# A two-block network on one core: some of TensorE's work moved to other places in its order, and one GpSimd product held back

## The chip, the cores and the metric

The kernel runs on one core of a Trainium2 chip. The metric is the device time of one execution in microseconds (us): the median of three runs before was 1147.24 (1146.61 to 1147.52). Everything is in one program with one instruction stream for each of five engines: TensorE (PE, and PEld for its weight loads), VectorE (DVE), ScalarE (ACT), GpSimd (POOL) and SyncE (SP), which issues most of the loads. The streams meet only through semaphores.

## What is computed

256 tokens of 1024 features pass through two blocks. The first is a mixer with four branches and a feed-forward; the second is an HGRN2 mixer, a feed-forward, an RG-LRU mixer and a feed-forward. Before each part stands an RMS norm, and after the last a final one. Cut to what matters here:

```python
def first_block(x, ...):
    h = rmsnorm(x, norm_mix)
    x = x + hybrid_mixer(h, ...)          # mamba2, moba, forgetting, sliding window; gates; @ w_out
    x = x + swiglu(rmsnorm(x, norm_ffn), w_gate, w_up, w_down)
    return rmsnorm(x, norm_final)

def second_block(x, ...):
    hn = rmsnorm_2(x, norm_mix[0]); x = x + hgrn2_mixer(hn, w_in, lb, norm_w, w_out)
    x = x + swiglu_2(rmsnorm_2(x, norm_ffn[0]), ffn_w_in[0], ffn_w_out[0])
    hn = rmsnorm_2(x, norm_mix[1]); x = x + rglru_mixer(hn, ...)
    x = x + swiglu_2(rmsnorm_2(x, norm_ffn[1]), ffn_w_in[1], ffn_w_out[1])
    return rmsnorm_2(x, norm_final)

# in hgrn2_mixer, at the end of each head:
#   o = o * rsqrt(mean(o*o)) * norm_w;  o = o * silu(g);  return o @ w_out
```

## The kernel before

**Matmuls in three parts.** Every fp32 product with a large weight is made of two halves of each operand: a high part (whi, hh, eh, gh, ch) rounded to fp32r and the rest (wlo, hl, el, gl, cl). TensorE computes high times high, weight's rest times high and weight's high times activations' rest into one PSUM bank. The weights stream through three slots in units of up to 1 MB. A unit j is loaded by SP in two halves into raw, ACT writes whi from it (L944), DVE (L1342), or for the second halves in the feed-forwards GpSimd (L1912), writes wlo, and then SP may load unit j+3. ACT may write whi of a slot only when TensorE has used the unit before in it (`used`).

**Two forms.** `still` (L480) keeps a weight tile in the array and moves the 256 tokens; a unit of 256 columns is two calls of 24 matmuls, L491 (high), L494 (weight's rest), L497 (activations' rest), in that order for each half of the unit. `moving` (L500) keeps the activations in the array and moves 512 columns of weights: L508 (high), L511 (weight's rest), L514 (activations' rest).

**A norm between two products.** `add_product` (L579) adds a product to x. Its four banks are 4, 6 (first columns) and 5, 7 (second columns) or the other way by token. Its last three units are run for the first two banks and then for the last two. DVE adds a bank to x and multiplies x by the norm's row into hn (`by_row`, L1354); ACT squares x for the mean; GpSimd makes the power; the factor per token is applied later. `transposes(c, e)` (L545) turns one half of hn, eight transposes (L554), into two banks; ACT copies them to hh (L976) and DVE writes hl (L1366). The first half is turned before the last unit's second banks, the second half in `project_pair` (L557). That function runs the two units behind a norm in halves: both units with features 0 to 511 (`part` 0), then `transposes(1, e)`, then unit one with features 512 to 1023, then the spreading of the norm's factors (diag by DVE at L1372, two matmuls with the identity at L574, copied by ACT at L984), then unit two. e numbers the norms: 2 before the first feed-forward, 3 before HGRN2 ("third norm", two norms in one), 5 and 7 before the other feed-forwards, 6 before the RG-LRU; 4 is HGRN2's own output norm.

**The start.** TensorE projects unit ("xbc", 0) (L640 to L649), then turns the 120 rows of small parameters (L656, "columns"), whose loads GpSimd issues, then projects the units ("xbc", 1 to 3). ACT copies the turned columns to vec (L1036), which the convolution on ACT (L1028) and DVE (L1472, L1474) needs.

**HGRN2.** Behind the projections of f and q, `level(j, i)` (L847, L842) computes score products for four pairs of heads at nine levels; between two levels of one pair DVE multiplies q and k by decays (L1749, L1756, L1757; they add one to s_q) and writes the selected scores (L1762). GpSimd multiplies the gates sgt by the output norm's weights in `scaled_gate` (L2059), four products. `turn_outputs` (L873) turns the mixed outputs og for `add_product(("ho",), ...)`: pieces 0 and 1 before it, pieces 2 and 3 inside it, before unit 2's first banks (`before_last`).

## Time and profile before

| | |
|---|---|
| median of three runs | 1147.24 us (1146.61 to 1147.52) |
| the profiled execution | 1146.94 us |
| its span, first to last instruction | 1145.7 us |
| PE (matmul) busy | 1126.2 us, 98% |
| DVE busy | 661.0 us, 58% |
| ACT busy | 575.6 us, 50% |
| POOL busy | 296.6 us, 26% |
| DMA, mean | 181 GB/s |
| mean granted TensorE clock | 0.998 |

Busy time is summed per engine; waits are idle time in front of an instruction, put down to the semaphore that came last. Matmuls are pipelined and the ends of their records are modelled, so two matmuls in the records overlap; the distance from one start to the next is what a matmul costs. A group of instructions in the timeline has one line: start, time from its first start to its last end, engine and line, tiles, count, and in brackets the engine's idle time before it with what ended it.

### The profile page before, as it was taken

What the parts mean: (1) busy time and instruction counts of PE and PEld (TensorE: products, weight loads), DVE (VectorE), ACT (ScalarE), POOL (GpSimd) and SP (SyncE); (2) the same over time, 40 slices, a digit from 0 to 9 for tenths busy, and PEclk for the clock granted to TensorE, in tenths of its full rate; (3) what the DMA queues carried; (4) which work ended last, traced back from release to release, by engine and by line L of the source; (5) the groups of instructions that cost most, each with busy time, mean ns of one, the idle gap of its engine ahead of it and who ended that gap; (6) DMA issues with size and microseconds to landing.
All of it is one profiled execution on the core that took longest, in us unless ns stands there. A gap on an engine that the chain in (4) does not pass through costs nothing.

```text
span 1145.7 us, 19296 instructions
## 1 busy us (share of the span) xinstructions
PE 1126.2 (98%) x8117; PEld 1046.1 (91%) x8117; DVE 661.0 (58%) x1034; ACT 575.6 (50%) x881; POOL 296.6 (26%) x193
## 2 busy tenths in 40 slices
PE   8999999999999999999999999999999999999997
PEld 6999989999989999888998889999889989999986
DVE  6655765677656454337897666434337796534324
ACT  6646555555435644436642445444435855444432
POOL 2023100000005444423321105444420002444440
PEclk9999999999999999999999999999999999999999
DMA  8679474544646666655553348665555354766550
GB/s 269 225 215 334 145 244 133 181 154 135 199 147 201 186 188 200 201 184 161 174 165 112 110 147 261 218 186 187 198 184 176 102 178 138 221 187 192 189 185 37
DMA packets 155152, 207.48 MB, mean 181 GB/s; under 512 B 9471, under 2 KB 128409, under 8 KB 155066
## 3 DMA queue, kind: packets, MB, share of 16 engines
q1 hardware_dynamic: 151274, 193.11, 53.5%
q0 software_dynamic: 3792, 13.15, 3.4%
q8 instruction: 64, 1.05, 0.4%
q14 instruction: 22, 0.18, 0.0%
HBM read 205.01 MB, written 4.24 MB: 183 GB/s over the span
## 4 chain that ended last, share of the span: by engine, by line
PE 89%; DVE 6%; ACT 2%; DMA 1%; issue 1%; POOL 0%; SPq 0%; DVEq 0%; ACTq 0%; POOLq 0%
PE bank L491 18%; PE bank L494 18%; PE bank L497 18%; PE bank L514 9%; PE bank L511 9%; PE bank L508 9%; PE bank L847 2%; DVE wlo L1342 2%; PE bank L773 1%; PE bank L783 1%; PE bank L795 1%; DMA area<-in_hgrn_lb 1%; PE bank L554 1%; DVE uc L1472 0%; ACT whi L944 0%
## 5 line engine op out<-in xcount | busy, mean ns | idle before, releaser
L1342 DVE TENSOR_TENSOR wlo<-raw,whi 128x1024 fp32r<-128x1024 f32 x275 | 339.3, 1261 | 227.7 <-ACT whi L944 226.7
L944 ACT ACTIVATE whi<-raw 128x1024 fp32r<-128x1024 f32 x362 | 360.7, 1044 | 110.4 <-PE bank L514 102.9
L1912 POOL TENSOR_TENSOR wlo<-raw,whi 128x1024 fp32r<-128x1024 f32 x87 | 223.2, 2566 | 256.0 <-ACT whi L944 256.0
L491 PE MATMUL bank<-hh,whi 128*128 128x256 f32 x1784 | 286.3, 281 | 1.7 <-ACT hh L976 1.7
L494 PE MATMUL bank<-hh,wlo 128*128 128x256 f32 x1784 | 281.7, 279 | 0.0
L497 PE MATMUL bank<-hl,whi 128*128 128x256 f32 x1784 | 281.5, 279 | 0.0
L491 PEld LDWEIGHTS bank<-hh,whi 128*128 128x128 f32 x1784 | 241.7, 188 | 6.7 <-issue 5.5
L494 PEld LDWEIGHTS bank<-hh,wlo 128*128 128x128 f32 x1784 | 240.8, 188 | 0.0
L497 PEld LDWEIGHTS bank<-hl,whi 128*128 128x128 f32 x1784 | 240.6, 188 | 0.0
L1919 POOL TENSOR_TENSOR st<-st,half 128x1 f32<-128x1 f32 x18 | 10.3, 580 | 334.6 <-DVE st L1359 310.3
L508 PE MATMUL bank<-whi,gh 128*128 128x512 f32 x264 | 81.5, 390 | 0.0
L514 PE MATMUL bank<-whi,gl 128*128 128x512 f32 x264 | 81.4, 389 | 0.0
L511 PE MATMUL bank<-wlo,gh 128*128 128x512 f32 x264 | 81.3, 389 | 0.0
L1171 ACT ACTIVATE sg<-sg 128x512 f32<-128x512 f32 x33 | 20.9, 632 | 95.6 <-DVE sg L1389 95.6
L1175 ACT ACTIVATE gh<-sg 128x512 fp32r<-128x512 f32 x33 | 20.8, 630 | 86.0 <-DVE sg L1705 86.0
L514 PEld LDWEIGHTS bank<-whi,gl 128*128 128x128 f32 x264 | 49.5, 188 | 10.4
L511 PEld LDWEIGHTS bank<-wlo,gh 128*128 128x128 f32 x264 | 49.5, 188 | 10.3
L508 PEld LDWEIGHTS bank<-whi,gh 128*128 128x128 f32 x264 | 49.2, 188 | 10.0
L1705 DVE TENSOR_TENSOR sg<-sg,bank 128x512 f32<-128x512 f32 x33 | 22.7, 687 | 57.4 <-PE bank L497 55.3
L1389 DVE TENSOR_TENSOR sg<-bank,bc_f 128x512 f32<-128x512 f32 x33 | 22.7, 688 | 43.9 <-PE bank L497 43.9
L969 ACT ACTIVATE bank<-x_sb 128x512 f32<-128x512 f32 x28 | 16.8, 598 | 56.5 <-DVE x_sb L1411 29.9
L1707 DVE TENSOR_TENSOR gl<-sg,gh 128x512 fp32r<-128x512 f32 x33 | 30.8, 932 | 23.3 <-ACT gh L1175 23.3
(308 smaller groups left out, 1224.7 us busy)
## 6 DMA issues: line engine op xcount, KB each, us to landing
raw<-in_ffn_w_in SPq DMA_DIRECT2D x88, 512.0 KB, 3.8
raw<-in_w_in SPq DMA_DIRECT2D x72, 512.0 KB, 5.0
raw<-in_ffn_w_out SPq DMA_DIRECT2D x44, 512.0 KB, 3.3
raw<-in_hgrn_w_in SPq DMA_DIRECT2D x32, 512.0 KB, 4.4
raw<-in_w_ffn_gate SPq DMA_DIRECT2D x22, 512.0 KB, 4.4
raw<-in_w_ffn_up SPq DMA_DIRECT2D x22, 512.0 KB, 4.3
raw<-in_w_ffn_down SPq DMA_DIRECT2D x22, 512.0 KB, 3.5
raw<-in_w_branch SPq DMA_DIRECT2D x16, 512.0 KB, 4.6
```

The lines of the kernel that those rows point to most:

```text
L491: T.matmul(out, wh[:, i, c], xh[:, k, :], start=first and (i, k) == pairs[0], stop=False)
L494: T.matmul(out, wl[:, i, c], xh[:, k, :], start=False, stop=False)
L497: t = T.matmul(out, wh[:, i, c], xl[:, k, :], start=False, stop=last and (i, k) == pairs[-1])
L508: T.matmul(out, xh[:, k, r], wh[:, i, c], start=first and i == 0, stop=False)
L511: T.matmul(out, xh[:, k, r], wl[:, i, c], start=False, stop=False)
L514: tok = T.matmul(out, xl[:, k, r], wh[:, i, c], start=False, stop=last and i == len(ks) - 1)
L847: tok = T.matmul(banks[b][:, 128 * (2 * h + t):128 * (2 * h + t) + 128], kj[:, h, c], qj[:, h, c], start=True, stop=True)
L944: A.activation(half_of(whi, j, h), half_of(raw, j, h), ACT.Copy).then_inc(s_hi[j % NS][h], 1)
L1342: V.tensor_tensor(half_of(wlo, j, h), half_of(raw, j, h), half_of(whi, j, h).bitcast(f32), ALU.subtract).then_inc(s_lo[j % NS][h], 1)
L1389: V.tensor_tensor(dst, two(bank_of("col", *key)[:, :]), bc[:, :].rearrange("p (o t) -> p o t", o=1).broadcast_to([128, 2, 256]), ALU.mult) ...
L1707: V.tensor_tensor(gl[:, 2 * j:2 * j + 2, :], two(s), gh[:, 2 * j:2 * j + 2, :].bitcast(f32), ALU.subtract).then_inc(s_gl, 1)
L1912: G.tensor_tensor(half_of(wlo, j, 1), half_of(raw, j, 1), half_of(whi, j, 1).bitcast(f32), ALU.subtract).then_inc(s_lo[j % NS][1], 1)
```

## The change

TensorE's order is changed at six points, and one wait is put before one GpSimd product. No matmul, transpose or DMA is added or removed.

1. Columns: the turning of the parameter rows is called after the first 24 matmuls of unit ("xbc", 1) instead of before them.
2. First rests: in w_out's product the first unit runs its L508 and L511 parts for all four banks, then the L514 parts for all four.
3. Norms' second turning: `transposes(1, e)` stands behind unit one's first half instead of behind both units' first halves (all five norms).
4. Third norm's factors: for e = 3 the spreading moves from before unit two's second half into it, behind the L494 part of its first 128 columns.
5. Last pieces: `turn_outputs((2, 3))` stands between the two banks of unit 1's first pass instead of before unit 2's.
6. GpSimd's last of the four gate products waits until s_q has its last value, that is, until DVE has done the last level's multiplications.

```diff
@@ still
+                    if inside is not None and of_half:
+                        inside()
                     for i, k in of_half:
                         tq.wait_ge(*lo(k))
                         t = T.matmul(out, wh[:, i, c], xl[:, k, :], ...)
@@ moving: each of the three loops now under "if 0 in parts", "if 1 in parts", "if 2 in parts"
@@ project_columns
                 for m in range(units[j][2] // 128):
                     t = still(...)
+                    if between is not None and m == 0:
+                        between()
@@ project_pair
                             tok = still(..., i0=4 * part, first=part == m == 0, last=part == m == 1,
+                                        inside=(lambda: spread_factors(e)) if part == i == 1 and m == 0 and e == 3 else None)
                         tok.then_inc(s_full[bs[i]], 1)
                         used[j, part] = ...
-                        if part == 1 and i == 0:
-                            turn(("fac", e), 4)
-                            tq.wait_ge(s_diag, SPREAD[e] + 2)
-                            tq.wait_ge(*free(("fac", e)))
-                            for t in range(2):
-                                tok = T.matmul(banks[4][:, 128 * t:128 * t + 128], diag[:, t, :], ident[:, :], start=True, stop=True)
-                            tok.then_inc(s_full[4], 1)
-                    if part == 0:
-                        transposes(1, e)
+                        if part == i == 0:
+                            transposes(1, e)
+                        if part == 1 and i == 0 and e != 3:
+                            spread_factors(e)
@@ add_product
                 for n in range(n_units - 3):
-                    part(n, 0)
-                    part(n, 1)
+                    for parts in ((0, 1), (2,)) if rests_last else ((0, 1, 2),):
+                        part(n, 0, parts)
+                        part(n, 1, parts)
                 for n in range(n_units - 3, n_units):
-                    if before_last is not None and n == n_units - 2:
-                        before_last()
-                    part(n, 0)
+                    part(n, 0, between=inside_second if n == n_units - 3 else None)
@@ start
             for j in range(1, 4):
-                project_columns(("xbc", j), 0)
+                project_columns(("xbc", j), 0, turn_columns if j == 1 else None)
@@ calls
-            add_product(("wo",), 4, eh, el, *of_norm(1), 2)
+            add_product(("wo",), 4, eh, el, *of_norm(1), 2, rests_last=True)
-            add_product(("ho",), 4, eh, el, *of_norm(4), 5, before_last=lambda: turn_outputs((2, 3)))
+            add_product(("ho",), 4, eh, el, *of_norm(4), 5, inside_second=lambda: turn_outputs((2, 3)))
@@ scaled_gate (GpSimd)
                 for t in range(2):
+                    if g2 == t == 1:
+                        gq.wait_ge(s_q, max(lev_q.values()))
                     gq.wait_ge(*evac("tok", "hg", g2, t))
```

## Rows read from the trace of the kernel before

**Rows 1.** The page: busy time of each engine, and its costliest TensorE line.
```profile
PE 1126.2 (98%) x8117; PEld 1046.1 (91%) x8117; DVE 661.0 (58%) x1034; ACT 575.6 (50%) x881; POOL 296.6 (26%) x193
...
L491 PE MATMUL bank<-hh,whi 128*128 128x256 f32 x1784 | 286.3, 281 | 1.7 <-ACT hh L976 1.7
```

**Rows 2.** Timeline at the start (start us, us, engine line, tiles, count, idle before).
```profile
14.60 4.62 DVE L1342 TENSOR_TENSOR wlo<-raw,whi 128x1024 fp32r<-128x1024 f32 x4
...
19.17 0.33 PE L656 MATMUL bank<-ident,area 120*128 120x120 f32 x1 [1.38 <-DMA area<-in_hgrn_lb]
...
19.53 0.27 ACT L1036 ACTIVATE vec<-bank 128x120 f32<-128x120 f32 x1 [1.11 <-PE bank L656]
```

**Rows 3.** Timeline at the unit z1.
```profile
44.79 2.36 DVE L1342 TENSOR_TENSOR wlo<-raw,whi 128x1024 fp32r<-128x1024 f32 x2 [1.65 <-ACT whi L944]
...
49.14 1.09 PE L511 MATMUL bank<-wlo,hh 128*128 128x512 f32 x4
```

**Rows 4.** Timeline of TensorE at w_out's first unit.
```profile
312.13 0.63 PE L511 MATMUL bank<-wlo,eh 128*128 128x512 f32 x2
313.95 0.74 PE L514 MATMUL bank<-whi,el 128*128 128x512 f32 x2 [1.19 <-DVE el L1662]
...
315.92 0.62 PE L508 MATMUL bank<-whi,eh 128*128 128x512 f32 x2
```

**Rows 5.** Timeline at the fourth norm (e = 5), one of five alike.
```profile
680.22 1.28 DVE L1354 TENSOR_TENSOR hn<-x_sb,wrow 128x512 f32<-128x512 f32 x2
...
681.78 0.63 PE L491 MATMUL bank<-hh,whi 128*128 128x256 f32 x4
...
684.61 1.04 PE L554 MATMUL bank<-ident,hn 128*128 128x128 f32 x8
...
686.73 0.63 PE L494 MATMUL bank<-hh,wlo 128*128 128x256 f32 x4
```

**Rows 6.** Timeline at the third norm (e = 3) and the first levels.
```profile
525.09 1.28 DVE L1354 TENSOR_TENSOR hn<-x_sb,wrow 128x512 f32<-128x512 f32 x2
...
525.97 0.63 PE L491 MATMUL bank<-hh,whi 128*128 128x256 f32 x4
...
529.43 1.08 ACT L976 ACTIVATE hh<-bank 128x512 fp32r<-128x512 f32 x2 [1.09 <-PE bank L554]
...
532.12 1.83 POOL L2068 MEMSET Ss<- 128x2048 f32 x1
...
532.63 1.47 DVE L1372 COPY diag<-st 128x128 f32<-128x128 f32 x2
...
534.16 0.71 PE L574 MATMUL bank<-ident,diag 128*128 128x128 f32 x4 [0.74 <-DVE diag L1372]
...
542.35 0.63 ACT L1203 ACTIVATE qT<-qT 128x512 f32<-128x512 f32 x1 [0.81 <-DVE qT L1389]
...
550.06 1.16 PE L847 MATMUL bank<-qT,kT 128*128 128x128 f32 x8 [0.15 <-DVE qT L1749]
```

**Rows 7.** One line's instructions (min/median/max ns), then the timeline at the last level.
```profile
L1756 DVE TENSOR_TENSOR qT<-qT,tot x24: 397/412/1431, 560.5 to 649.5; 128x256 f32<-128x256 f32 x24
...
649.38 1.27 POOL L2059 TENSOR_TENSOR sgt<-sgt,nw 128x512 f32<-128x512 f32 x1 [1.52 <-ACT sgt L1226]
649.51 1.42 DVE L1756 TENSOR_TENSOR qT<-qT,tot 128x256 f32<-128x256 f32 x1 [2.84 <-PE bank L847]
...
651.32 0.71 PE L842 MATMUL bank<-qT,kT 128*128 128x128 f32 x4 [0.98 <-DVE kT L1757]
```

**Rows 8.** Timeline of TensorE at the last pieces' turning.
```profile
662.95 1.03 PE L880 MATMUL bank<-ident,og 128*128 128x128 f32 x8
...
664.87 0.62 PE L511 MATMUL bank<-wlo,eh 128*128 128x512 f32 x2
```

**Rows 9.** Timeline in the first feed-forward: a split on GpSimd and its first reader.
```profile
346.18 2.95 POOL L1912 TENSOR_TENSOR wlo<-raw,whi 128x1024 fp32r<-128x1024 f32 x1 [5.90 <-ACT whi L944]
...
351.16 0.63 PE L494 MATMUL bank<-hh,wlo 128*128 128x256 f32 x4
```

More of the change, by code:

```diff
@@ L478, in next_bank, with still @@
                 return rot_banks[0][(rotation[0] - 1) % len(rot_banks[0])]
-            def still(out, j, m, xh, xl, ks, hi, lo, i0=0, first=True, last=True):
+            def still(out, j, m, xh, xl, ks, hi, lo, i0=0, first=True, last=True, inside=None):
                 wh, wl = whole(whi, j), whole(wlo, j)
@@ L498, in still, with moving @@
                 return t
-            def moving(out, j, t, xh, xl, ks, c0, n, hi, lo, first=True, last=True):
+            def moving(out, j, t, xh, xl, ks, c0, n, hi, lo, first=True, last=True, parts=(0, 1, 2)):
                 wh, wl = whole(whi, j), whole(wlo, j)
@@ L504, in moving @@
                 half_k = units[j][1] // 2
-                for i, k in enumerate(ks):
-                    tq.wait_ge(*hi_set(j, i // half_k))
-                    tq.wait_ge(*hi(k))
-                    T.matmul(out, xh[:, k, r], wh[:, i, c], start=first and i == 0, stop=False)
-                for i, k in enumerate(ks):
-                    tq.wait_ge(*lo_set(j, i // half_k))
-                    T.matmul(out, xh[:, k, r], wl[:, i, c], start=False, stop=False)
-                for i, k in enumerate(ks):
-                    tq.wait_ge(*lo(k))
-                    tok = T.matmul(out, xl[:, k, r], wh[:, i, c], start=False, stop=last and i == len(ks) - 1)
+                if 0 in parts:
+                    for i, k in enumerate(ks):
+                        tq.wait_ge(*hi_set(j, i // half_k))
+                        tq.wait_ge(*hi(k))
+                        tok = T.matmul(out, xh[:, k, r], wh[:, i, c], start=first and i == 0, stop=False)
+                if 1 in parts:
+                    for i, k in enumerate(ks):
+                        tq.wait_ge(*lo_set(j, i // half_k))
+                        tok = T.matmul(out, xh[:, k, r], wl[:, i, c], start=False, stop=False)
+                if 2 in parts:
+                    for i, k in enumerate(ks):
+                        tq.wait_ge(*lo(k))
+                        tok = T.matmul(out, xl[:, k, r], wh[:, i, c], start=False, stop=last and i == len(ks) - 1)
                 return tok
@@ L555, in transposes, with spread_factors @@
                     tok.then_inc(s_full[b], 1)
+            def spread_factors(e):
+                turn(("fac", e), 4)
+                tq.wait_ge(s_diag, SPREAD[e] + 2)
+                tq.wait_ge(*free(("fac", e)))
+                for t in range(2):
+                    tok = T.matmul(banks[4][:, 128 * t:128 * t + 128], diag[:, t, :], ident[:, :], start=True, stop=True)
+                tok.then_inc(s_full[4], 1)
             def project_pair(keys, e):
@@ L586, in part @@
                         b, name = 4 + 2 * t + c, ("add", e, t, c)
-                        if n == 0:
+                        if n == 0 and 0 in parts:
                             turn(name, b, n_units if b == 7 else 1)
```

27 lines of the change are left out of this document (15 added, 12 removed).

## The prediction

> **What bounds the kernel now.** I read the page first. TensorE (PE) is busy for 1126.2 of 1145.7 us and the next engine for 661.0 [rows 1], so nothing can be won by making another engine cheaper. What can be won is TensorE's own idle time, 19.5 us in all, part of it at the very start where the first loads land. I then took the waits of TensorE, longest first, and looked at each in the timeline, measuring from start to start, because the ends of matmuls are modelled. The cadence comes from rows: 24 matmuls of 256 columns take 684.61 - 681.78 = 2.83 us, 0.118 each [rows 5], and eight of 512 columns with one restart take 315.92 - 313.95 = 1.97, about 0.23 each [rows 4]. Eight transposes span 1.04 us, the last one's own 0.27 in it, so they start 0.11 apart and take 0.88 [rows 5]. Every edit puts work that is issued anyway into one of these holes. So I ask for each: how long is the hole, is the work put in ready by then, and what is late next.
>
> **1, columns' turning.** TensorE stands 1.38 us until the last of the parameter rows has landed, and turns at 19.17 [rows 2]. By cadence the unit before ends 0.16 after the idle time begins, so the hole is 1.54. The second unit's split is done long before: the four passes of DVE from 14.60 take 4.62, and the first two of them are its own [rows 2]. The change runs 24 matmuls (2.83) first, so TensorE reaches the turning at 19.17 - 1.54 + 2.83 = 20.46, 1.3 after the landing. That removes 1.54. But ACT copies the columns at 19.53 only because of this turning [rows 2], and its queue, convolution and splits behind it, moves 1.29 later while TensorE moves 1.54 earlier. In the timeline each of its waits there is one for DVE's convolution, which hangs on ACT in turn, so the lag holds up to the splits of the unit z1: DVE's two passes from 44.79 take 2.36 and end at 47.15; TensorE wants the second half's rest part two matmuls after 49.14, at 49.6 [rows 3]. Slack 2.45, used 1.54 + 1.29 = 2.83, so a new stall of 0.4 stands there. After that unit ACT's waits are for TensorE, and the lag ends. Net -1.1, between 0 (the lag costs more than I see) and -1.5 (none of it).
>
> **2, first rests.** At unit 0 of w_out, TensorE needs el 0.46 after 312.13 and gets it at 313.95 [rows 4]: a hole of 1.36, and about 0.05 of restart. With all hi and lo parts of the four banks first, 16 matmuls (3.7 us) stand before the first rest, which covers it. Nothing waits for the single banks of unit 0 but the slot's release, which comes at the unit's end either way. -1.4, bounds -1.2 and -1.5.
>
> **3, norms' second turning.** In the pair of units behind a norm TensorE turns hn's second half at 684.61 and starts the second group of four matmuls after it at 686.73 [rows 5]. Of these 2.12, four matmuls are 0.47 and the transposes 0.88; 0.77 is waiting for ACT's hh. This stands at five norms (the page sums only 1.7 for all, since it misses the wait inside the group [rows 1]). Turning 2.83 earlier puts 24 matmuls behind the transposes. For that hn must be there: DVE's two products end at 680.22 + 1.28 = 681.50, and TensorE arrives at 681.78, 0.28 later [rows 5]. ACT is idle then and waits for just these banks. ACT's and DVE's steps behind (splits, factor) come earlier than before, so the factor's spreading, left where it is at four norms, finds its input. 4 x 0.75 = -3.0, bounds -2.7 and -3.1; the LRU's chain on DVE hangs on ACT's reading of the spread factor and moves with it.
>
> **4, third norm (hgrn): turning and factors together.** Here hn ends at 525.09 + 1.28 = 526.37, while TensorE would arrive at 525.97 [rows 6]: it stalls 0.35 in the new place. The factor is late too: two copies of diag take 1.47 (their kind takes about 0.2 elsewhere), beside GpSimd's memset of Ss (1.83 from 532.12), and the spreading starts at 534.16 after 0.74 idle [rows 6]. ACT stood idle 1.09 before its hh at 529.43 [rows 6]; with the banks there earlier it starts up to that much sooner, and DVE reaches diag about 0.9 earlier, at 531.7. With the copies short again the factor is there before 532.3, and the spreading, now eight matmuls into the next unit, starts at about 533.85. TensorE alone would gain 1.2. What is late next is the first level: from the spreading, ACT and DVE run one chain (factor copy, split, two table loads, sigmoid, SiLU) that ends at 542.35 + 0.63 = 542.98 and feeds the level; at 550.06 the next level waits for DVE already [rows 6]. That chain is 534.16 to 542.98 = 8.8 long and moves only with its start, 0.3. Net -0.3, bounds 0 and -0.5.
> The row shows copies that ran until the memset ended. The Trainium skill, page SBUF — State Buffer, section Who interferes with whom, says that for the port pair the two engines share, issue order decides and the later one blocks fully. By that rule the 0.3 hangs on diag being issued first; if the memset is, the sum below is 7.1 instead of 7.4.
>
> **5, GpSimd's last gates later.** GpSimd's product of 1.27 from 649.38 lies over DVE's L1756, which takes 1.42 instead of its median 0.412, and TensorE waits 0.98 for what follows [rows 7]. With the product behind the last level's semaphore, DVE's two steps end 1.0 earlier, and so does the wait. Behind the waiting instruction on GpSimd stand only two small powers of the output norm, needed about 4 us later; the product ends near 651.7. -1.0, bounds -0.7 and -1.1.
>
> **6, last pieces' turning.** From the eight transposes at 662.95 to the second pair's start at 664.87 it is 1.92; less 0.46 and 0.88, 0.58 is waiting [rows 8]. One bank's six matmuls (1.36) now cover ACT's copy, which takes 1.08 after the first four transposes. ACT and DVE reach it behind their splits of the last unit, just in time. -0.6, bounds -0.3 and -0.6.
>
> Nothing is added: the same matmuls, transposes and DMAs are issued, SP's queue is untouched, and its loads follow the splits. **Sum:** 1.1 + 1.4 + 3.0 + 0.3 + 1.0 + 0.6 = 7.4. Against the profiled execution, 1146.94 (span 1145.7 and 1.2 around it), that makes 1139.5; the median of the three runs is 0.3 above the profiled one, so **1139.8**. The bounds alone span -4.9 to -8.7, 1142.3 to 1138.5.
>
> **Rivals.** (a) The covers are shorter than they look in the places with thin margins: the columns' lag on ACT costs 1 more, the third norm gives nothing, the last pieces half, the last gates half. Then 7.4 - (1.0 + 0.3 + 0.3 + 0.5) = 5.3 is left, or 4.3 if last gates and last pieces give nothing and the second turnings 0.2 less: **1141.9 to 1142.9**. For it: the columns' lag is read off a chain of some twenty steps, and 0.3 at the third norm rests on 0.4 of timing. Against it: the other rows have slack.
> (b) TensorE reaches the turning before hn at all norms, as it does at the third. Then the stall only changes its place and the 3.0 are gone: **1142.8**. Against it: 0.28 of slack at the norm shown, and both ends of that slack hang on TensorE's own sum, so they move together.
> (c) The order does not do what it says: other engines carry the pace at later joints (DVE at 550.06, and in the LRU stage) and take back nearly everything, **1146 to 1147**. Against it: those engines' work is released by TensorE's results, so it moves up with them.
> (d) Slower. In the three feed-forwards GpSimd makes 87 of the splits. The one from 346.18 takes 2.95 and ends at 349.13; TensorE needs it at 351.16 [rows 9], slack 2.03. Moving DVE's steps up at each norm sets a new phase between DVE's and GpSimd's products, which block one another (item 5: one collision cost 1.0). If the splits lose 2.03 each nothing happens; from there each 0.1 lost costs 8.7 in all, so at 0.085 the gain is gone, and at 0.2 the kernel takes 1139.8 + 17.4 = **1157**. Against it: the slack is twice the dearest collision in the rows.
>
> **How the numbers follow.** Forecast, 1138.4 to 1141.3: 0.69. (a) 0.17, (b) 0.04, (c) 0.06, (d) 0.04. The range 1138.2 to 1142.9 takes in the forecast, (a) and (b), 0.90 with some doubt about terms that I have not seen, so 8 in 10. A measurement of this kernel can tell about 0.2% from no change, 2.3 us: faster than 1144.9 is the forecast, (a) and (b), 0.90; (c) is no change, 0.06; (d) slower, 0.04.
>
> **What the profile after would show.** TensorE's waits for area, for el at w_out's first unit, for hh behind the transposes and for kT at the last level are gone, each by its price. A new wait of about 0.4 for wlo near 47, one of about 0.35 for hn near 524, and one near 540 for q at the first level. L1756's longest drops to about 0.4. TensorE's busy time stays, the granted clock stays. I am wrong if waits for wlo from GpSimd appear in the feed-forwards, if the copy of the columns makes several units of the first stage wait, or if the second turning waits for hn at more than one norm.

## The result, and the profile after

| | before | after |
|---|---|---|
| median | 1146.92 us of 4 runs (1145.89 to 1147.52) | **1140.30 us** of 4 runs (1139.91 to 1140.68) |
| the profiled execution, its span | 1146.94, 1145.7 | 1139.91, 1138.7 |
| mean granted TensorE clock | 0.998 | 1.0 |

The ratio is 0.9942, 95% interval 0.9929 to 0.9954: faster by 0.6%. The forecast was 1139.8 in a range of 1138.2 to 1142.9. With the lines that were added, L491, L494, L497 are now L492, L495, L500; L508, L511, L514 are L512, L516, L520; the transposes of a norm L562, the spreading L570, the levels L857 and L862, DVE's splits L1357.

The first two lines are the page of the kernel after (its busy times, beside [rows 1], and the line that answers to L491), and the rest its view of TensorE's waits (in total, times, longest).

```profile
PE 1123.5 (99%) x8117; PEld 1045.2 (92%) x8117; DVE 659.0 (58%) x1034; ACT 575.0 (50%) x881; POOL 295.6 (26%) x193
...
L492 PE MATMUL bank<-hh,whi 128*128 128x256 f32 x1784 | 285.2, 281 | 0.0
```

```profile
PE bank L516 <- DVE wlo L1357: 1.6, 3, 0.7
...
PE bank L862 <- issue: 0.7, 1, 0.7
PE bank L862 <- DVE qT L1764: 0.4, 1, 0.4
...
PE bank L562 <- DVE hn L1369: 0.2, 1, 0.2
PE bank L570 <- DVE diag L1387: 0.2, 1, 0.2
```

The waits for the parameter row, for el, for hh behind the norms' transposes, for eh behind the last pieces' (0.34 at 664.33 before) and for kT are gone, and the idle time in front of L492, 1.7 before, is 0.0. New are hn at L562 and the first line of L862, and L516 has a third place. One of 0.2 for hh at the very start (L653), far from the edits, is new in this execution too.

To see what each edit gave I compared where the same matmul (the nth with its tiles and columns) starts in the two traces. Its distance is what has been gained up to there.

| stretch | edit | before, after (start, us) | gained so far | by this edit | predicted |
|---|---|---|---|---|---|
| to 28 us | columns | 28.06, 26.52 | 1.54 | 1.54 | 1.54 |
| to 55 | (given back at z1) | 54.98, 53.98 | 1.00 | -0.54 | -0.4 |
| 121 to 136 | none | 135.96, 135.33 | 0.63 | **-0.37** | 0 |
| to 320 | first rests | 320.01, 317.86 | 2.15 | 1.51 | 1.4 |
| to 350 | second turning, e = 2 | 349.98, 347.05 | 2.93 | 0.78 | 0.75 |
| 520 to 560 | third norm | 560.03, 556.89 | 3.14 | 0.21 | 0.3 |
| 640 to 655 | GpSimd's last gates | 654.99, 650.86 | 4.13 | 1.00 | 1.0 |
| to 670 | last pieces | 669.89, 665.15 | 4.74 | 0.61 | 0.6 |
| to 700 | second turning, e = 5 | 700.01, 694.50 | 5.51 | 0.77 | 0.75 |
| to 900 | second turning, e = 6 | 899.98, 893.71 | 6.27 | 0.77 | 0.75 |
| to 1000 | second turning, e = 7 | 999.98, 992.95 | 7.03 | 0.78 | 0.75 |

Five of the six edits came out within 0.15 of their terms. (The changed execution stood 0.06 behind when the first stretch began, at 13 us, so the columns' edit removed 1.60: the hole of 1.54 and a restart of TensorE.) Two lines of the table need an explanation: the third norm's 0.21, and 0.37 that got lost between 121 and 136 us, where nothing was changed.

**The edits in the timeline after.** Columns, and the wait at z1 (answering to [rows 2, 3]):

```profile
20.52 0.27 PE L670 MATMUL bank<-ident,area 120*128 120x120 f32 x1
...
20.82 0.27 ACT L1051 ACTIVATE vec<-bank 128x120 f32<-128x120 f32 x1 [2.33 <-PE bank L670]
...
46.08 2.36 DVE L1357 TENSOR_TENSOR wlo<-raw,whi 128x1024 fp32r<-128x1024 f32 x2 [1.65 <-ACT whi L959]
...
48.50 0.73 PE L516 MATMUL bank<-wlo,hh 128*128 128x512 f32 x2 [0.23 <-DVE wlo L1357]
```

The turning is at 20.52 (20.46 forecast) and waits for nothing. ACT's copy moved from 19.53 to 20.82 and, 25 us and some twenty steps further on, DVE's passes of z1 from 44.79 to 46.08: 1.29 both, as the prediction had it. They end at 48.44, and TensorE goes on at 48.50. The record shows 0.23 idle, since the modelled end of the matmul before covers the rest; from start to start it is 0.54: 0.40 in front of the matmul, 0.10 in the distance to the next, and 0.04 a group earlier, at L512.

First rests [rows 4]: the L514 part for four banks is now one group behind 16 others, and has no wait.

```profile
314.23 0.62 PE L516 MATMUL bank<-wlo,eh 128*128 128x512 f32 x2
314.69 1.98 PE L520 MATMUL bank<-whi,el 128*128 128x512 f32 x8
```

The norm e = 5 [rows 5]: from the transposes to the second group behind them 1.35 (678.39 - 677.04), where it was 2.12.

```profile
677.04 1.04 PE L562 MATMUL bank<-ident,hn 128*128 128x128 f32 x8
...
678.39 0.63 PE L495 MATMUL bank<-hh,wlo 128*128 128x256 f32 x4
```

The last pieces [rows 8]: six matmuls of one bank stand behind the eight transposes, and 2.24 (659.71 - 657.47) go by up to the next bank with no wait.

```profile
657.47 1.03 PE L895 MATMUL bank<-ident,og 128*128 128x128 f32 x8
```

The last level [rows 7]. GpSimd's product now starts behind DVE's two, at 647.21, and L1771 takes 0.43; TensorE's wait is gone.

```profile
646.37 0.43 DVE L1771 TENSOR_TENSOR qT<-qT,tot 128x256 f32<-128x256 f32 x1 [2.83 <-PE bank L862]
...
647.19 0.71 PE L857 MATMUL bank<-qT,kT 128*128 128x128 f32 x4
647.21 1.27 POOL L2077 TENSOR_TENSOR sgt<-sgt,nw 128x512 f32<-128x512 f32 x1 [2.49 <-DVE kT L1772]
```

The third norm and the first levels [rows 6]:

```profile
523.50 0.98 PE L562 MATMUL bank<-ident,hn 128*128 128x128 f32 x7 [0.19 <-DVE hn L1369]
...
528.74 2.44 DVE L1387 COPY diag<-st 128x128 f32<-128x128 f32 x2
...
529.20 1.83 POOL L2086 MEMSET Ss<- 128x2048 f32 x1
...
531.24 0.71 PE L570 MATMUL bank<-ident,diag 128*128 128x128 f32 x4 [0.16 <-DVE diag L1387]
...
540.16 1.13 PE L862 MATMUL bank<-qT,kT 128*128 128x128 f32 x8 [0.67 <-issue]
...
547.13 1.16 PE L862 MATMUL bank<-qT,kT 128*128 128x128 f32 x8 [0.40 <-DVE qT L1764]
```

DVE reaches diag 0.96 earlier than before (528.74 + 2.93 gained up to there = 531.67, against 532.63), but the copies now take 2.44 and end at 531.18. Before they ended at 534.10, and 534.10 - 2.93 is 531.17. They end where GpSimd's memset ends, and that has not moved.

**The lost 0.37.** The unit from 120 us in both kernels (before, then after): the same 96 matmuls with the same data.

```profile
120.85 0.62 PE L494 MATMUL bank<-hh,wlo 128*128 128x256 f32 x4
121.30 0.62 PE L497 MATMUL bank<-hl,whi 128*128 128x256 f32 x4
```

```profile
119.86 0.63 PE L495 MATMUL bank<-hh,wlo 128*128 128x256 f32 x4
120.33 0.63 PE L500 MATMUL bank<-hl,whi 128*128 128x256 f32 x4
```

Four matmuls take 0.453 before and 0.471 after: 113.3 or 117.8 ns each, the same for all 94 distances of the stretch, 0.42 in all, of which 0.05 comes back by 136 us. There is no wait in it, and the granted clock is 1.00, the level of 2.4 GHz, in both.

```profile
120.00:131.00 11.00, 11.00 (x98) 10.71 (x95) 7.44 (x20) 6.38 (x16) 2.19 (x3) 1.00 0.15 57
```

```profile
120.00:131.00 11.00, 11.00 (x95) 10.87 (x95) 7.46 (x23) 7.39 (x17) 2.19 (x3) 1.00 0.21 59
```

(Busy time in the stretch of PE, PEld, DVE, ACT, POOL, then the clock, the DMA share and GB/s.) So there are two paces for the same instructions at the same clock. Which one a stretch has is read off its first ten distances and holds to its end.

### The profile page after: what moved, and what is told of

Read it like the earlier page. It is cut to its first block, busy times and chain, and to the rows that moved or that the text cites. A ratio compares the mean times of both kernels' runs of the same rounds, so it can differ in the third digit from the quotient of the medians.

```text
span 1138.7 us, 19297 instructions
## 1 busy us (share of the span) xinstructions
PE 1123.5 (99%) x8117; PEld 1045.2 (92%) x8117; DVE 659.0 (58%) x1034; ACT 575.0 (50%) x881; POOL 295.6 (26%) x193
## 3 DMA queue, kind: packets, MB, share of 16 engines
q8 instruction: 64, 1.05, 0.4%
## 4 chain that ended last, share of the span: by engine, by line
PE 87%; DVE 8%; ACT 3%; issue 1%; DMA 0%; POOL 0%; SPq 0%; DVEq 0%; ACTq 0%; POOLq 0%
PE bank L492 18%; PE bank L495 18%; PE bank L500 18%; PE bank L520 9%; PE bank L516 9%; PE bank L512 9%; DVE wlo L1357 3%; PE bank L862 2%; PE bank L788 1%; ACT whi L959 1%; PE bank L798 1%; DVE area L1487 1%; PE bank L562 1%; PE bank L810 1%; DVE uc L1487 0%
## 5 line engine op out<-in xcount | busy, mean ns | idle before, releaser
L1357 DVE TENSOR_TENSOR wlo<-raw,whi 128x1024 fp32r<-128x1024 f32 x275 | 336.9, 1253 | 232.1 <-ACT whi L959 231.2
L492 PE MATMUL bank<-hh,whi 128*128 128x256 f32 x1784 | 285.2, 281 | 0.0
L495 PE MATMUL bank<-hh,wlo 128*128 128x256 f32 x1784 | 281.7, 279 | 0.0
L500 PE MATMUL bank<-hl,whi 128*128 128x256 f32 x1784 | 281.6, 279 | 0.0
L492 PEld LDWEIGHTS bank<-hh,whi 128*128 128x128 f32 x1784 | 241.4, 188 | 3.3 <-issue 2.7
L495 PEld LDWEIGHTS bank<-hh,wlo 128*128 128x128 f32 x1784 | 240.8, 188 | 0.0
L500 PEld LDWEIGHTS bank<-hl,whi 128*128 128x128 f32 x1784 | 240.6, 188 | 0.0
L512 PE MATMUL bank<-whi,gh 128*128 128x512 f32 x264 | 81.4, 390 | 0.0
L516 PE MATMUL bank<-wlo,gh 128*128 128x512 f32 x264 | 81.4, 389 | 0.0
L520 PE MATMUL bank<-whi,gl 128*128 128x512 f32 x264 | 81.3, 389 | 0.0
L1186 ACT ACTIVATE sg<-sg 128x512 f32<-128x512 f32 x33 | 20.8, 632 | 95.6 <-DVE sg L1404 95.6
L1190 ACT ACTIVATE gh<-sg 128x512 fp32r<-128x512 f32 x33 | 20.8, 630 | 86.0 <-DVE sg L1720 86.0
L520 PEld LDWEIGHTS bank<-whi,gl 128*128 128x128 f32 x264 | 49.5, 188 | 10.4
L516 PEld LDWEIGHTS bank<-wlo,gh 128*128 128x128 f32 x264 | 49.6, 188 | 10.3
L512 PEld LDWEIGHTS bank<-whi,gh 128*128 128x128 f32 x264 | 49.2, 188 | 9.9
```

The lines of the kernel that those rows point to most:

```text
L492: T.matmul(out, wh[:, i, c], xh[:, k, :], start=first and (i, k) == pairs[0], stop=False)
L495: T.matmul(out, wl[:, i, c], xh[:, k, :], start=False, stop=False)
L500: t = T.matmul(out, wh[:, i, c], xl[:, k, :], start=False, stop=last and (i, k) == pairs[-1])
L512: tok = T.matmul(out, xh[:, k, r], wh[:, i, c], start=first and i == 0, stop=False)
L516: tok = T.matmul(out, xh[:, k, r], wl[:, i, c], start=False, stop=False)
L520: tok = T.matmul(out, xl[:, k, r], wh[:, i, c], start=False, stop=last and i == len(ks) - 1)
```

## The experiments

Each is an edit of the changed kernel unless it says otherwise, and its trace was compared with that kernel's at the same matmuls.

**e1, the second turning put back at four norms.**

```diff
-                        if part == i == 0:
+                        if part == i == 0 and e == 3:
                             transposes(1, e)
...
+                    if part == 0 and e != 3:
+                        transposes(1, e)
```

> The changed kernel (1140.3 us) with the second turning put back behind both first halves at the four norms other than the third. Theory of the sum: the wait for ACT's hh behind the eight transposes comes back, 0.75 at each of the four, +3.0 in all: 1143.3, and TensorE's starts behind the four norms are later by 0.75 each. Rival (other engines set the pace at later joints): under 1.0 of it shows, 1140.3 to 1141.3.

Measured 1143.07 (1142.89 to 1143.66, 6 runs). In the trace TensorE falls back by 0.77, 0.77, 0.77 and 0.76 at the four norms, and nowhere else by more than the 0.2 of pace. At the end the two traces are 3.3 apart, 0.2 of it pace, and the medians 2.8, for 3.0 forecast. The row at e = 5:

```profile
680.85 1.03 PE L562 MATMUL bank<-ident,hn 128*128 128x128 f32 x8
682.23 0.90 PE L492 MATMUL bank<-hh,whi 128*128 128x256 f32 x4 [0.34 <-ACT hh L993]
```

So no other engine takes the term back, and rival (c) of the prediction falls.

**e2, three edits undone: columns, GpSimd's last gates, last pieces.**

```diff
+            turn_columns()
             for j in range(1, 4):
-                project_columns(("xbc", j), 0, turn_columns if j == 1 else None)
+                project_columns(("xbc", j), 0)
...
-                        gq.wait_ge(s_q, max(lev_q.values()))
...
-                    part(n, 0, between=inside_second if n == n_units - 3 else None)
+                    if inside_second is not None and n == n_units - 2:
+                        inside_second()
+                    part(n, 0)
```

> The changed kernel with three of its edits undone at once, each in its own stretch of the trace: the columns turned before unit (xbc, 1), GpSimd's last gate product not held back, and the last pieces turned before unit 2 of the product. Theory of the sum: the wait for the last parameter row (1.5) comes back and the wait of 0.5 for wlo at z1 goes, net +1.0; the wait for kT at the last level comes back, +1.0; the wait for the pieces +0.6. Together +2.6: 1142.9. Rival for the columns: ACT's lag is not what makes the wait at z1, it stays at 0.5 and the net is +1.5. Rival for the last gates: DVE's two products are slow for another reason than GpSimd's beside them, they stay at 0.4 with it back, and +0.0.

Measured 1142.99 (1141.57 to 1145.11, 10 runs), +2.7 for +2.6. By stretch: columns +0.73, last gates +0.98, last pieces +0.62. These make 2.3, and the traces end 2.63 apart; 0.2 of the rest is pace at 548 us, so a part of the agreement in the total is luck. The collision is back as it was:

```profile
647.20 1.27 POOL L2077 TENSOR_TENSOR sgt<-sgt,nw 128x512 f32<-128x512 f32 x1 [1.50 <-ACT sgt L1244]
647.32 1.43 DVE L1774 TENSOR_TENSOR qT<-qT,tot 128x256 f32<-128x256 f32 x1 [2.83 <-PE bank L865]
...
649.14 0.71 PE L860 MATMUL bank<-qT,kT 128*128 128x128 f32 x4 [0.98 <-DVE kT L1775]
```

With the columns back in their old place the wait at z1 is gone (its 0.54 is won back there), and DVE's passes of z1 start at 44.53 in place of 46.08: ACT's lag makes it. The columns gave less than 1.0 because TensorE itself started 0.5 to 0.6 later in this execution while the row landed at 18.85, so the hole was smaller: what this edit is worth depends on two moments that differ from execution to execution.

**e3, the third norm as before** (both the turning and the spreading).

```diff
-                        if part == i == 0:
+                        if part == i == 0 and e != 3:
                             transposes(1, e)
-                        if part == 1 and i == 0 and e != 3:
+                        if part == 1 and i == 0:
                             spread_factors(e)
+                    if part == 0 and e == 3:
+                        transposes(1, e)
```

> The changed kernel with the third norm as it was before: turning behind both first halves and the factors' spreading ahead of unit two. Theory: the chain from the spreading through ACT's sigmoids and SiLU to the first level sets the time there, so the gain that is lost is small, +0.2 to +0.3: 1140.5 to 1140.6, and the first level no longer waits for q. Rival: TensorE's own order sets it and the whole 1.2 is lost: 1141.5. In either case diag's two copies take 1.3 to 1.5 beside GpSimd's memset of Ss, as they did in the kernel before.

Measured 1140.34 (1140.03 to 1140.54, 4 runs): no difference from 1140.30. Its trace ends 0.32 behind that of the changed kernel, but it has no stretch at 113.3 ns between 541 and 553, and the changed kernel's profiled execution has two. With e1, which has the new third norm and 117.8 in both stretches, the pace can be left out: against the kernel before, e1 stands at 2.26 at 520 us and 2.24 at 640, e3 at 2.97 and 2.95. Old or new order, the third norm gives the same, and the rival of a whole 1.2 falls. Item 4 is worth 0.0; the 0.21 of the table is pace. As expected the first level doesn't wait, since TensorE is late itself:

```profile
531.20 0.71 PE L570 MATMUL bank<-ident,diag 128*128 128x128 f32 x4 [0.75 <-DVE diag L1389]
```

**e5, GpSimd's memset behind diag.**

```diff
+            gq.wait_ge(s_diag, SPREAD[3] + 2)
             G.memset(Ss[:, :, :], 0.0).then_inc(s_z, 1)
```

> The changed kernel (1140.3 us) with one wait more on GpSimd: the memset of Ss waits until DVE has made both halves of diag. In the changed kernel the two copies are issued at 528.74 and 528.87, 0.46 and 0.33 ahead of the memset (529.20 to 531.03), and both end with it, at 531.11 and 531.18. Theory 1 (GpSimd's memset holds DVE's copies up though they were issued first): the copies take about 0.2 each and diag is there near 529.1, TensorE's wait of 0.3 ahead of the spreading is gone, the chain to q's SiLU starts 0.3 earlier and TensorE's wait at the first level shrinks by as much: 1140.0, a gain of 0.3 in the stretch to 545. Theory 2 (what holds them is the issuing of the two loads ahead of the memset, 528.06 to 529.21): the copies end at about 529.3. Theory 3 (they are slow for another reason): they still take 2.3, and nothing moves.

Measured 1139.76 (1139.11 to 1139.94, 4 runs). Theory 1 holds, theory 2 falls: the copies run inside GpSimd's issuing of a load and take 0.36 together.

```profile
528.33 0.55 POOL L2085 DMA_DIRECT2D nw<-in_hgrn_norm  x1
528.40 0.36 DVE L1387 COPY diag<-st 128x128 f32<-128x128 f32 x2
...
530.34 0.60 PE L570 MATMUL bank<-ident,diag 128*128 128x128 f32 x4
```

The wait ahead of the spreading is gone and the stretch from 518 to 547 is 0.65 shorter, up to 0.2 of it pace (113.3 ns from 524 to 530). So the memset held the copies up for 2.1 us, although their records start 0.46 and 0.33 ahead of it. The rule quoted in the prediction, from the Trainium skill, page SBUF — State Buffer, section Who interferes with whom, says that the one issued first has the ports and the later one blocks. Taken by the starts of the records it does not describe this row: the one that starts earlier waited. Spans of GpSimd are rough in these records, so whether the memset was in truth issued first, and the rule holds after all, stays open.

**e6, the columns turned after 12 matmuls,** from inside `still`, instead of after 24.

```diff
-                    if between is not None and m == 0:
-                        between()
...
+                    if half_way is not None and h == 0:
+                        half_way()
```

> The changed kernel with the columns turned after the first 12 matmuls of unit (xbc, 1) instead of after 24. TensorE reaches the turning 1.41 after the unit's start instead of 2.83, at about the moment at which the last row lands, and ACT's copy of the columns keeps its old time. Theory (ACT's lag behind TensorE is what makes the new wait of 0.5 at z1): lag 1.4 in place of 2.8 against a slack of 2.45, so the wait at z1 is gone and a wait of 0.1 stands at the turning: 0.4 faster in the stretch to 60 us, 1139.9. Rival (the wait at z1 comes from elsewhere): it stays, and with the 0.1 at the turning the time is 1140.3 to 1140.4.

Measured 1139.67 (1139.10 to 1140.62, 4 runs). The turning was at 19.68 with no wait, the row having landed at 17.67, and the wait at z1 is gone: TensorE enters the stretch 0.58 later than in the changed kernel and leaves it 0.03 later. That alone proves little: TensorE had started about 0.6 later in this execution and is at the matmul at 48.63, behind the 48.44 at which DVE was done in the changed kernel. What decides is DVE's own time at z1, 0.82 earlier than in the changed kernel, as the turning is 0.84 earlier:

```profile
45.26 2.36 DVE L1357 TENSOR_TENSOR wlo<-raw,whi 128x1024 fp32r<-128x1024 f32 x2 [1.65 <-ACT whi L959]
```

In all fourteen profiled executions these passes start 25.56 to 25.63 behind the turning, wherever the turning stands (18.90 to 20.84). The rival falls.

**e8, the work of f and q ahead of splits at the third norm, on ACT and DVE, with e5's edit.**

```diff
                 aq.wait_ge(*full("fac", e))
                 A.activation(bc[:, :], banks[4][:, 0:256], ACT.Copy)...
+                if e == 3:
+                    evacs[0]()
+                    evacs[1]()
+                    split(j + 3, 0)
+                    split(j + 3, 1)
+                    return
                 split(j + 3, 0)
                 evacs[0]()
```

(and the same behind `split_to(j + 2)` on DVE)

> The changed kernel with the memset behind diag as in the run above, and on ACT and DVE at the third norm alone the work of f and q (f times the factor, table, sigmoids, q times the factor, table, SiLU) ahead of the splits of the unit two further on. Theory (the chain from the spreading to q's SiLU sets when the first level may start): SiLU ends 1.5 to 2 earlier, near 538, and TensorE's wait of 0.8 at the first level is gone; the next wait, 0.5 for q's decay at the next level, has a chain of its own and stays: 1139.2 to 1139.6. Rival 1: that chain moves up too and its wait goes as well: 1138.7 to 1139.1. Rival 2: the splits, now 2 us later, become late for the unit hq 1 at 541: nothing gained or slower, 1140 to 1141.5.

Measured 1138.97 (1138.85 to 1139.45, 4 runs). The median lies in rival 1's range, but the trace shows the theory's case: the first level waits no more, TensorE is 1.25 earlier there, and 0.44 is given back at the next level, whose wait stays and is longer:

```profile
542.55 0.68 DVE L1416 TENSOR_TENSOR fT<-bank,bc_hg 128x512 f32<-128x512 f32 x1
...
545.64 0.68 DVE L1776 TENSOR_TENSOR qT<-qT,fT 128x512 f32<-128x512 f32 x1
...
546.38 0.82 PE L862 MATMUL bank<-qT,kT 128*128 128x128 f32 x5 [0.71 <-DVE qT L1776]
```

The product that TensorE waits for, L1776, has had its bank since 540.0 (TensorE's group for it ran from 538.95 for 1.05). It stands in DVE's order behind f's work for the second unit (L1416 and four operations, with 1.22 of waiting for ACT among them).

**e10, the edits of e5, e6 and e8 together, and L1776 ahead of that work** (the diff shows the last alone).

```diff
                 use(("hf", j))
+                if j == 1:
+                    levels("hf", j)
                 f_of(j)
-                levels("hf", j)
+                if j > 1:
+                    levels("hf", j)
```

> The changed kernel (1140.3 us) with four edits: the columns turned after 12 matmuls; GpSimd's memset of Ss behind diag; at the third norm, on ACT and DVE, the work of f and q ahead of the splits of the unit two further on; and on DVE the first level's product and selection ahead of f's work for the second unit, since TensorE's next wait (0.71 at 546.4 in the run with q first) is for that product, which is queued behind f's four operations. Theory (each of these stretches gives what it showed alone and nothing behind them takes it back): the wait at z1 is gone for 0.1 at the turning, -0.4; no wait at the first level, -1.2 with the memset's part; no wait at the second level, -0.5 more. 1140.3 - 2.1 = 1138.2. Rival (the work put off, the splits or the second unit's f and q, becomes late instead): the gain stays at that of the run with q first and the columns, 1138.6 to 1139.2.

**e11, the changed kernel again, on the same chip.**

> The changed kernel itself once more, beside the kernel of the run above, so that the two can be compared on one chip. The same as in its first runs: 1140.3, 1139.9 to 1140.7, and 0.9942 of the kernel before.

Measured: e10 1138.78 (1138.22 to 1139.16, 5 runs), the changed kernel 1139.97 (1139.94 to 1140.77, 5 runs; 0.9937 of the kernel before, 0.9924 to 0.9949). From 518 to 556 us e10 is 1.8 faster; the pace gives each of the two about 0.2 there that the other lacks, e10 at 524 and the changed kernel at 548. But it lost 0.8 at the turning, and that puts the profiled execution (1138.75) in the rival's range; the rival's reason, late work at the third norm, does not show:

```profile
20.21 0.32 PE L670 MATMUL bank<-ident,area 120*128 120x120 f32 x1 [0.63 <-DMA area<-in_hgrn_lb]
```

The parameter row landed at 20.16 in this execution. In the twelve profiled executions other than e7's and e9's it landed between 17.34 (e8) and 20.16: 19.12 in the kernel before, 18.91 in the changed one. I had taken the one value for a constant. After 12 matmuls, at 19.1 to 19.7, TensorE is there too early for four of them (19.87, 20.01, 20.03, 20.16). And 20.16 is not the latest: in e7's execution, whose start is the changed kernel's, the row landed at 20.79, and TensorE waited for it even after 24 matmuls, 0.5 by the records, so "never waited" in the next expectation does not hold for all executions.

**e12, e10 with the turning after 20 matmuls,** behind the L495 part of the second half of the unit's first 128 columns.

```diff
-                    if half_way is not None and h == 0:
+                    if half_way is not None and h == 1:
```

> The kernel of the run with four edits together, with the columns turned after 20 matmuls of unit (xbc, 1) instead of 12. In the ten executions profiled so far the last parameter row landed between 17.34 and 20.16 us; after 12 matmuls TensorE is at the turning at 19.4 to 19.7 and waited 0.8 in the execution in which the row landed at 20.16; after 24 it is there at 20.2 to 20.6 and never waited, but ACT's lag costs 0.5 at z1. After 20 it is there at 20.0 to 20.2. Theory: a wait of at most 0.2 at the turning in the latest landings, and ACT's lag of 2.36 just fits in the slack of 2.45 at z1, so at most 0.1 stands there: in the stretch to 60 us 0.4 less than the changed kernel whenever the row lands, 1138.2. Rival (it makes no difference on average, since most executions land early): 1138.6 to 1138.9, as after 12.

Measured **1138.01** (1137.63 to 1138.35, 5 runs), 0.992 of the kernel before, interval 0.9907 to 0.9934. None of its runs comes near the nine of the changed kernel (1139.91 to 1140.77), though those were taken in other comparisons. In the stretch to 60 us it is 0.40 faster than the changed kernel, as its theory had it. But the row landed at 19.11 in this execution, so no profile shows the place after 20 matmuls meeting a late landing. The view of its waits (its lines behind those for the first loads; left out are one of 0.6 for hh at the start and one of 0.2 for hn) has none left at z1, at the third norm's spreading and at the levels:

```profile
PE bank L518 <- DVE wlo L1363: 1.4, 2, 0.7
PE bank L514 <- DVE cl L1885: 1.0, 1, 1.0
PE bank L764 <- ACT ring L1142: 0.7, 1, 0.7
```

**e4, e7, e9: what sets the pace.** e4 makes TensorE wait for its own last matmul:

```diff
                         if part == 1 and i == 0 and e != 3:
+                            if e == 7:
+                                tq.wait_ge(*used[j, part])
                             spread_factors(e)
+                            if e == 2:
+                                tq.wait_ge(*full("fac", e))
...
+                    if f == 1:
+                        tq.wait_ge(*used[unit_at["g", f, j], 1])
                     project_columns(("u", f, j), e)
```

> Matmuls of 256 columns start either 117.8 or 113.3 ns apart in both traces, the same pace from a stretch's first matmul to its last; which one differs between the two kernels for the same instructions (120 to 131 us: 113.3 before, 117.8 after; 541 to 553 us: 117.8 before, 113.3 after). The changed kernel with TensorE made to wait for its own last matmul at a few places: in the first feed-forward once, between the spreading of the factors and the long stretch of 982 matmuls; in the second ahead of ten units, every second one; in the third once, ahead of the spreading. Theory 1 (a stretch has the fast pace when the array has been emptied ahead of it): stretches behind the waits run at 113.3, each wait costs 0.1 to 0.3, and the long stretches are 4.4 us shorter each: 1140.3 - 13 + 3 = 1130. Theory 2 (the pace is left as it falls by the moment at which a wait ends): some of the ten at 113.3, some not. Theory 3 (it has nothing to do with waits): all at 117.8, and only the waits' price shows, 1142 to 1143.

Measured 1143.86 (1143.59 to 1144.14, 8 runs): all twelve stretches behind the waits are at 117.8, and each wait costs 0.32 to 0.33. That is theory 3, and theories 1 and 2 fall. Its 1142 to 1143 was too low by the price of a wait, assumed at 0.1 to 0.3: twelve of them make 3.9. The same kernel has 113.3 at 120 us, where nothing was changed.

e7 puts a list of twenty kinds of dummy matmuls and waits (three of them repeat another) ahead of units, three times each:

```diff
+                        poke(e, *used[unit_at[last], 1])
                         project_columns(key, e)
```

> A look at what sets the pace of 113.3 or 117.8 ns. The changed kernel with small dummy matmuls (into a free bank, read by nobody) and waits of TensorE for its own last matmul ahead of 60 units in the three feed-forwards, twenty kinds three times in different orders: nothing; 1, 2, 4 or 6 transposes of 128 columns; 1, 2 or 4 matmuls of 128 columns; one matmul on 64 rows alone, or with 1, 4 or 6 transposes behind; a wait for its own last matmul alone or ahead of these. Each unit's 48 matmuls show the pace. Theory A (what precedes a unit sets its pace, as 6 transposes behind matmuls on 64 rows do in all 15 places of the attention stage): the same kinds give 113.3 in all three feed-forwards, and the others 117.8. Theory B (only the moment matters): no kind gives the same in all three. Theory C: all at 117.8. The time is about 1140.3 plus 25 for the dummies, less 0.2 for each unit at 113.3.

Measured 1173.76 (one run). Three of 60 units are at 113.3, each of another kind (one transpose behind the wait; one matmul on 64 rows and a transpose; six transposes), and each of these kinds gave 117.8 in its other places. So theory A falls. Theory B asked for more than was seen, since the other kinds gave 117.8 all three times; that the moment decides is what is left, and isn't shown.

e9 copies what stands ahead of the ten fast places of the attention stage:

> A second look at the pace. The changed kernel with copies of what stands ahead of the ten places of the attention stage that had 113.3 ns in every execution so far, put ahead of the 60 units of the feed-forwards as dummies into free banks: pairs of matmuls on 64 rows each, of 128 and 256 columns, with 6, 2 or no transposes behind them; the pairs of 256 alone; the pairs with the output's halves split by columns; all of it behind TensorE's wait for its own last matmul; and nothing, twelve kinds, five times each. Theory A (the sequence sets the pace): the full sequence gives 113.3 in all its five places. Theory B (the moment decides, and the attention stage only repeats its own moments): no kind gives 113.3 in more than two of five. The time is about 1140 plus 60 to 80 for the dummies.

Measured 1221.61 (one run). All 60 are at 117.8, so theory A falls here too. From 1.5 us ahead of the unit the copy is exact, with every distance the same within 1 ns; below first its row at 346 us, then the changed kernel's at 146:

```profile
346.76 0.93 PE L851 MATMUL bank<-ident 64*128 64x128 f32 x8
347.62 0.88 PE L861 MATMUL bank<-ident 128*128 128x128 f32 x6
348.25 0.71 PE L492 MATMUL bank<-hh,whi 128*128 128x256 f32 x4
348.80 0.63 PE L495 MATMUL bank<-hh,wlo 128*128 128x256 f32 x4
349.27 0.40 PE L500 MATMUL bank<-hl,whi 128*128 128x256 f32 x2
```

```profile
146.54 0.93 PE L788 MATMUL bank<-qkv 64*128 64x128 f32 x8
147.40 0.87 PE L798 MATMUL bank<-ident,ring 128*128 128x128 f32 x6
148.03 0.70 PE L492 MATMUL bank<-hh,whi 128*128 128x256 f32 x4
148.57 0.62 PE L495 MATMUL bank<-hh,wlo 128*128 128x256 f32 x4
149.02 0.39 PE L500 MATMUL bank<-hl,whi 128*128 128x256 f32 x2
```

Both have 0.63 from the transposes to the first group. Behind it four matmuls take 0.47 in the one (349.27 - 348.80) and 0.45 in the other. So the sequence of distances in the 1.5 us ahead doesn't set the pace, and the cause stays open. The dummies worked on the identity and not on the stage's own data, and that is one thing that the copy didn't copy.

## Why the prediction was right, and where it was not

- **The reading of the bound** held. 19.5 us of TensorE's idle time became 15.2 by the page, and its busy time fell by 2.7, which I had said would stay. The two sum to the 7.0. The ends of matmuls are modelled, so a part of each wait is booked as busy time of the matmul before it: at a norm's turning 0.77 is gone from start to start, of which the records called 0.34 idle (1.7 for five). Whoever sums the idle column of the kernel before gets too small a gain; measuring from start to start was the right way.
- **1, columns.** The hole (1.54), the new arrival (20.52 for 20.46) and ACT's lag (1.29 for 1.29, over 25 us) came out. (The unit before ends 0.16 ahead of the start of the idle time, and not after it as the prediction says; the 1.54 is right.) The wait at z1 was 0.54 for 0.4: the arithmetic of ready times gave its 0.40 and leaves out TensorE's restart, 0.10. What I missed is that the landing of the row is no constant (17.3 to 20.8 in fourteen executions).
- **2, first rests.** 1.51 for 1.4, at the bound. In the trace before, the hole is 1.35, and the first distance behind it 0.340 where 0.233 is the rule there, so the restart is 0.11 and not 0.05; the last 0.05 is pace, 0.233 for 0.227 in the ten distances that follow. This edit alone was not undone in a run, so its term rests on the two traces.
- **3, second turning.** 0.775 for 0.75 at each of four norms, and e1 gives it back one for one. Rival (b), a stall for hn everywhere, has its one case at the third norm, as forecast (L562, 0.19 by the records, 0.35 from start to start for 0.35).
- **4, third norm.** Predicted 0.3, worth 0.0. The step that failed is "with the copies short again". I had DVE at diag 0.9 earlier (0.96 measured) and thought that this gets it ahead of GpSimd's memset. It does, by 0.46, and it does not help. The sentence behind it, that without short copies the sum is 7.1, was the right branch in its size; whether for the reason given there, the memset issued first, is open. That the chain from the spreading to q's SiLU is what limits the stretch was right: TensorE alone won 0.94 (forecast 1.2) up to 540 us (540.01 before, 536.14 after, 3.87 of which 2.93 was there already) and lost it at the first two levels (540.16, the wait "issue" of 0.67, and 547.13), and e5 and e8, which shorten just this chain, are the edits that gain there.
- **5, last gates.** 1.00 for 1.0; e2 brings the collision back to the digit. The forecast that L1756's longest would drop to 0.4 was wrong: the row gave only the maximum, and two of the 24 took 1.43. The other, at 616 us before and 613 after, is still there and TensorE doesn't wait for it.
- **6, last pieces.** 0.61 for 0.6.
- **Rival (d)**, GpSimd's splits thrown out of phase: TensorE has no wait for wlo in the feed-forwards after either.
- **The sum.** 7.4 forecast; 7.03 in the profiled execution; 6.6 between the medians of the first comparison and 7.2 (1147.15 less 1139.97) in e11's. The difference of the traces is two things: 0.3 at the third norm, and a pace that took 0.37 at 120 us and gave 0.2 at 548. The terms that were too low by 0.1 make up the rest. Errors of both signs met here, so that the median came within 0.5 of the forecast is in part luck. The pace is a property of an execution and not of the edit: at 120 us two of the fourteen executions profiled have 113.3, the kernel before and e4. It swung the comparison by as much as some of the edits are worth. One sum of the prediction is wrong: the terms' upper bounds add to 8.3 and not 8.7, so the bounds alone end at 1138.9 and not 1138.5. The measured time lies inside both.

## What to carry to other kernels

Where one engine is busy 98% of the time, list its waits, measure each from start to start, and ask of work already issued what fits in front: such terms came out within 0.15 us here, and added up. A wait that goes makes the next one visible, and it is often an order on the feeding engine that is easy to turn: at the levels, three short edits on ACT, DVE and GpSimd gave another 1.8. A moment that comes from a load (17.3 to 20.8 us here) wants several executions before an order is fitted to it: the place that fitted one execution cost 0.8 in another.

## What the runs showed of the hardware that was not expected

- **Two paces at one clock.** Matmuls of 256 columns with new weights each start 113.3 or 117.8 ns apart, at a granted clock of 1.00, over whole stretches of 22 to 982 matmuls. In all fourteen profiled executions ten places of the attention stage (148, 175, 182 to 275 us) are fast, and in the twelve without dummies the long stretches of the feed-forwards are slow. In six other places, at 13, 25, 120, 524, 541 and 548 us, it differs from execution to execution: of those twelve they are fast in two, one, two, two, three and three, and e11, the same kernel as after, has it at 548 alone, where after has 541 and 548. Neither emptying the array (e4), nor the kind of work ahead (e7), nor the same sequence of distances (e9) sets it. By these figures the three long stretches of 982 would be 4.4 us shorter each at the fast pace (an estimate, 982 times 4.5 ns), more than everything in this change; how to get it stays open.
- **A copy held up by a memset whose record starts after it.** Two DVE copies of 128x128 took 0.36 together beside GpSimd's issuing of a load, and 2.44 where the memset of 128x2048 began 0.46 behind the first of them: they end within 0.15 of the memset's end (531.18 and 531.03). GpSimd's records are rough, so which of the two was issued first isn't shown.
- **The pace counts only where TensorE isn't waited down.** Beside e11, which has the slow pace from 541 to 546 us, the changed kernel's first execution has won 0.15 by 545 and nothing by 547, where both wait for DVE's qT.
